# A decoder block on one core: first token tiles loaded in halves and multiplied in passes, softmax blocks taken from last to first, causal mask in the decay row

## What is computed

```
h = layer_norm(x)
hg_q, hg_f, hg_i, hg_g, fx_q, fx_k, fx_v, fx_f, gate_a, gate_b = split(h @ w_in)
y_a = hgrn2(...)            # 4 heads, a gated linear recurrence
y_b = fox(fx_q, fx_k, fx_v, fx_f)
      # 8 heads of 64: logits = q k / 8 + c[t] - c[s], c = cumsum(log sigmoid(fx_f + bias)),
      # s <= t only, softmax, times v
merged = sigmoid(gate_a) * (y_a @ w_a) + sigmoid(gate_b) * (y_b @ w_b)
h = layer_norm(alpha * h + merged @ w_o)
h = layer_norm(alpha * h + relu(h @ w_ff1)**2 @ w_ff2 + sigmoid(h @ w_pg) * (p @ w_p))
```

## Time and profile before

| what | value |
|---|---|
| runs | 1638.04 us median of 3 (1636.09 to 1638.63) |
| the profiled execution | 1637.65 us, its span 1635.8 us |
| PE, PEld | busy 1588.1 us (97%), 1325.1 us (81%) |
| DVE, ACT, POOL | busy 1150.4 us (70%), 744.0 us (45%), 694.2 us (42%) |
| DMA | 208.51 MB, mean 127 GB/s |
| chain of waits | PE 83%, DVE 5%, ACT 4%, DMA 2%, POOL 2%, issue 2% |

### The profile page before, as it was taken

How to read it: one execution, slowest core, us unless ns; L and a number is a source line. 1 busy time by engine, 2 the same in 40 slices (tenths; PEclk the granted TensorE clock), 3 DMA queues, 4 the chain that set the end, 5 groups by cost and what they waited for, 6 DMA issues and landing times.

```text
span 1635.8 us, 21111 instructions
## 1 busy us (share of the span) xinstructions
PE 1588.1 (97%) x7800; PEld 1325.1 (81%) x7800; DVE 1150.4 (70%) x1724; ACT 744.0 (45%) x1162; POOL 694.2 (42%) x487
## 2 busy tenths in 40 slices
PE   6999999999999999999999989999999999999996
PEld 4888888888888887888887868888888888888886
DVE  8558878437767668656336879986666579857977
ACT  3245454327888774511233644445444553433342
POOL 5222221522333145564443597765566323223334
PEclk9999999999999999999999999999999999999999
DMA  8211110101010143521333435554444598867672
GB/s 295 77 42 38 27 39 27 39 29 38 27 53 27 39 117 97 147 78 52 122 120 118 164 126 183 182 195 143 159 168 152 185 330 254 272 199 238 194 204 104
DMA packets 220693, 208.51 MB, mean 127 GB/s; under 512 B 9000, under 2 KB 190504, under 8 KB 218544
## 3 DMA queue, kind: packets, MB, share of 16 engines
q1 hardware_dynamic: 217424, 196.09, 38.7%
q10 hardware_dynamic: 3168, 11.08, 1.7%
HBM read 160.96 MB, written 46.17 MB: 127 GB/s over the span
## 4 chain that ended last, share of the span: by engine, by line
PE 83%; DVE 5%; ACT 4%; DMA 2%; POOL 2%; issue 2%; SPq 0%; DVEq 0%; ACTq 0%; POOLq 0%
PE dense L969 7%; PE dense L971 7%; PE dense L973 7%; PE dense L979 4%; PE dense L1315 3%; PE dense L1317 3%; PE dense L1316 3%; PE dense L1395 3%; PE dense L1396 3%; PE dense L1397 3%; PE mixA L1106 2%; PE dense L1047 2%; PE dense L1049 2%; PE dense L1048 2%; PE mixA L1315 2%
## 5 line engine op out<-in xcount | busy, mean ns | idle before, releaser
L969 PE MATMUL dense<-parts 128*128 128x512 f32 x528 | 183.3, 409 | 1.6 <-DVE page L2090 0.9
L943 POOL TENSOR_TENSOR parts<-page,parts 128x512 fp32r<-128x512 f32 x52 | 88.9, 1733 | 208.1 <-ACT parts L1909 208.1
L862 POOL TENSOR_TENSOR parts<-page,parts 128x512 fp32r<-128x512 f32 x108 | 156.3, 1469 | 44.9 <-ACT parts L1788 41.6
L971 PE MATMUL dense<-parts 128*128 128x512 f32 x528 | 174.0, 391 | 0.0
L973 PE MATMUL dense<-parts 128*128 128x512 f32 x528 | 173.3, 390 | 0.0
L854 POOL CAST parts<-page 128x1024 fp32r<-128x1024 f32 x43 | 49.3, 1145 | 287.4 <-PE dense L973 192.4
L905 POOL TENSOR_TENSOR page<-page 128x512 f32<-128x512 f32 x80 | 122.6, 1532 | 59.8 <-PE dense L1317 25.2
L913 POOL TENSOR_TENSOR parts<-page,parts 128x512 fp32r<-128x512 f32 x80 | 114.8, 1437 | 55.4 <-ACT parts L1835 50.6
L1919 ACT CAST parts<-page 128x1024 fp32r<-128x1024 f32 x56 | 58.8, 1055 | 142.8 <-DVE page L2614 123.2
L973 PEld LDWEIGHTS dense<-parts 128*128 128x128 f32 x528 | 99.1, 188 | 21.8
L971 PEld LDWEIGHTS dense<-parts 128*128 128x128 f32 x528 | 99.1, 188 | 21.0
(11 more groups left out here) (298 smaller groups left out, 4315.8 us busy)
## 6 DMA issues: line engine op xcount, KB each, us to landing
page<-in_w_ff SPq DMA_DIRECT2D x104, 512.0 KB, 6.0
page<-in_w_in SPq DMA_DIRECT2D x120, 256.0 KB, 3.2
page<-act_scratch SPq DMA_DIRECT2D x56, 512.0 KB, 5.7
act_scratch<-page SPq DMA_DIRECT2D x16, 1024.0 KB, 3.9
act_scratch<-page SPq DMA_DIRECT2D x16, 768.0 KB, 7.0
page<-in_w_o SPq DMA_DIRECT2D x32, 256.0 KB, 3.1
h_scratch<-page ACTq DMA_DIRECT2D x8, 512.0 KB, 3.5
page<-c_scratch SPq DMA_DIRECT2D x8, 512.0 KB, 5.0
```

The costliest lines, as they stand in the source:

```text
L862: ins = nc.gpsimd.tensor_tensor(R(lo, at, HALF), F(raw_page(c), at, HALF), R(hi, at, HALF).bitcast(F32), ALU.subtract)
L969: mm(o, whi, x_, start=first, stop=False)
L971: mm(o, whi, x_, start=False, stop=False)
```

## The change

It has two parts.

The start. Token tiles 0 and 1, ln0_g and ln0_b are loaded in column halves, the first half from SyncE's queue, the second from ScalarE's, ahead of all weights; weight chunks 0 and 2 then follow on SyncE's queue, 1 and 3 on ScalarE's. The first value tiles are multiplied in passes (`first_values(t, n, ks)`): n = 0 is high by high, 1 low tokens by high weights, 2 high tokens by low weights. ScalarE's order becomes: chunk 0, tile 0's high part, chunks 1 to 3, tile 1's high part, tile 2's. VectorE's low part of tile 1 moves between the two passes of tile 2's norm. The semaphores x0_in, g0_in and b0_in are others' that are used again with shifted counts.

The softmax stage. The blocks of a head go from 7 down to 0 (`block_of(G) = 7 - G % 8`), the pairs from (7, 6) down to (1, 0). The 64 mask matmuls are gone; VectorE adds the mask to the diagonal square of the decay row itself, in place, one block ahead (`mask_diagonal(G + 1)`), which fits since the blocks that follow end below that square. The exception for G % 8 == 7 on ScalarE is gone.

```diff
+def block_of(G):
+    return 7 - G % 8
 def turn_pieces(G):
-    return [(0, 4), (4, G % 8 + 1)] if G % 8 >= 5 else [(0, G % 8 + 1)]
+    i = block_of(G)
+    return [(0, 4), (4, i + 1)] if i >= 5 else [(0, i + 1)]
...
@@ SyncE
-            sp.dma_start(F(PG_X), x_t[0]).then_inc(x_in[0], 16)
+            sp.dma_start(F(PG_X, 0, HALF), x_t[0][:, 0:HALF]).then_inc(x_in[0], 16)
+            sp.dma_start(F(PG_G0, 0, HALF), row(ln0_g)[:, 0:HALF]).then_inc(g0_in, 16)
+            sp.dma_start(F(PG_B0, 0, HALF), row(ln0_b)[:, 0:HALF]).then_inc(b0_in, 16)
+            sp.dma_start(F(PG_X + 1, 0, HALF), x_t[1][:, 0:HALF]).then_inc(x_in[1], 16)
             for c in range(C_END):
+                if c in (1, 3):
+                    continue
...
-                if c == 3:
-                    for t in range(4, TT):
+                if c == 2:
+                    for t in range(2, TT):
@@ TensorE, start
+            def first_values(t, n, ks):
+                j = JOB["vhg", t]
+                out1 = dense[SET[j]][:, 0:HALF]
+                x_, base = (XHI, XLO, XHI)[n], (WHI, WHI, WLO)[n]
+                for k in ks:
+                    if t == 0 and n != 1 and k % 2 == 0:
+                        pe.wait_ge((w0_hi, None, w0_split)[n], k // 2 + 1)
+                    ins = mm(out1, R(x_ + k, t * P, P), R(base + k // 2, (k % 2) * HALF, HALF),
+                             start=n == 0 and k == 0, stop=n == 2 and k == KD - 1)
+                if n == 2 and ks[-1] == KD - 1:
+                    end(ins, j)
             turn_tokens(0)
-            for t in range(TT):
+            begin(JOB["vhg", 0])
+            pe.wait_ge(h_hi, 1)
+            first_values(0, 0, every)
+            pe.wait_ge(h_split, 1)
+            first_values(0, 1, every)
+            first_values(0, 2, range(0, 2))
+            turn_tokens(1)
+            first_values(0, 2, range(2, 4))
+            begin(JOB["vhg", 1])
+            pe.wait_ge(h_hi, 2)
+            first_values(1, 0, every)
+            pe.wait_ge(h_split, 2)
+            first_values(1, 1, every)
+            first_values(0, 2, range(4, 6))
+            turn_tokens(2)
+            first_values(1, 2, early)
+            first_values(0, 2, late)
+            first_values(1, 2, late)
+            for t in range(2, TT):
@@ TensorE, scores
-                mm(mixA[:, L - P:L], identb[:, :], causal[:, :], start=False, stop=True,
-                   ).then_inc(qk_done, 1)
@@ ScalarE, start
+            act.dma_start(F(PG_X, HALF, HALF), x_t[0][:, HALF:]).then_inc(x0_in, 16)
+            act.dma_start(F(PG_G0, HALF, HALF), row(ln0_g)[:, HALF:]).then_inc(g0_in, 16)
             act.dma_start(ident[:, :], c_ident).then_inc(ident_in, 16)
+            act.dma_start(F(PG_B0, HALF, HALF), row(ln0_b)[:, HALF:]).then_inc(b0_in, 16)
+            act.dma_start(F(PG_X + 1, HALF, HALF), x_t[1][:, HALF:]).then_inc(x1_in, 16)
+            for c in (1, 3):
+                for i in range(2):
+                    act.dma_start(F(PG_W0 + c, i * HALF, HALF), w_views["in"][:, 2 * c + i, C_HI:C_HI + HALF],
+                                  ).then_inc(w0_landed[c], 16)
@@ ScalarE, softmax
-                if 2 <= G < 66 and G % 8 == 7:
-                    high_parts(G)
                 if 1 <= G < 65:
                     divide(G)
-                if 2 <= G < 66 and G % 8 != 7:
+                if 2 <= G < 66:
                     high_parts(G)
@@ VectorE, start
-            tokens_norm(0)
-            tokens_stats(1)
-            norm_begin(F(PG_X + 1), F(PG_X + 1), 1, F(PG_G0), 1)
-            tokens_low(0)
-            norm_end(F(PG_X + 1), 1, F(PG_B0), 1).then_inc(h_ready, 1)
-            for t in range(1, TT):
+            norm_begin(F(PG_X), F(PG_X), 0, F(PG_G0), 0)
+            dve.wait_ge(b0_in, 32)
+            norm_end(F(PG_X), 0, F(PG_B0), 0).then_inc(h_ready, 1)
+            for t in range(1, 3):
+                tokens_stats(t)
+                norm_begin(F(PG_X + t), F(PG_X + t), t % 2, F(PG_G0), t)
+                tokens_low(t - 1)
+                norm_end(F(PG_X + t), t % 2, F(PG_B0), t).then_inc(h_ready, 1)
+            for t in range(2, TT):
                 if t + 1 < TT:
                     tokens_stats(t + 1)
                     tokens_norm(t + 1)
@@ VectorE, softmax
+            def mask_diagonal(G):
+                hh = G // 8
+                if G % 8 == 0:
+                    dve.wait_ge(negc_in[hh % 2], 16 * (hh // 2 + 1))
+                if G == 0:
+                    dve.wait_ge(c_ready, 1)
+                square = F(PG_NEGC[hh % 2], block_of(G) * P, P)
+                then(V.tensor_tensor(square, square, causal[:, :], ALU.add))
...
+                if G < 63:
+                    mask_diagonal(G + 1)
                 if G >= 8 and G % 8 in (1, 2) and G // 8 + 1 < NFX:
```

More of the change, by code:

```diff
@@ L1464, in _ @@
                 nc.scalar.copy(R(WHI + j), F(PG_W0 + j)).then_inc(w0_hi, 1)
-                if j == 1:
+                if j == 0:
                     tokens_high(0)
                     rstd_estimate(1)
-            for t in range(1, TT + 1):
+            rstd_estimate(2)
+            tokens_high(1)
+            rstd_estimate(3)
+            tokens_high(2)
+            store_values(PG_VHG, "vhg", 0, 0)
+            store_values(PG_VHG, "vhg", 1, 0)
+            for t in range(3, TT + 1):
                 if t + 1 < TT:
@@ L1673, in _ @@
                     act.wait_ge(pv_done, m + 1)
[L1674 removed]
+                    nc.scalar.copy(F(PG_YB[m // 8], (3 - m % 4) * 2 * P, 2 * P)[own, :], o_bank(m)[other, :]).then_inc(o_moved, 1)
                 if G >= 8 and G % 8 == 1 and G // 8 + 1 < NFX:
```

66 lines of the change are left out of this document (28 added, 38 removed).

## The result

The change makes the kernel slower: 1656.96 us in the median of 5 runs (1653.16 to 1658.42) against 1636.67 for the kernel before on the same chip, ratio 1.0119, 95% interval 1.0108 to 1.013. The direction was forecast, the size was not: +20.3 us where +4.6 was forecast, above the range of 1633 to 1648. The profiled execution took 1657.6 us (span 1655.7), 19.95 more than the one before.

What follows compares the result with a forecast made beforehand. TensorE's waits were taken as the bound: at the start, in the gate stage and in softmax operand gaps. Masks -3.5, order +6.8 and start +1.3 made +4.6 on 1637.65: 1642.2, say 1642.0 us, range 1633 to 1648.

Steps and rivals of the forecast that it cites:

- hidden by sum: Softmax stage: VectorE's mask additions, 8 x 0.3 us a head, fit its spare time, counting only where its queue is awaited.
- Masks, -3.5: Softmax stage: dropping 64 mask matmuls at 0.055 us each saves TensorE 3.5 us on the path.
- VectorE has 7 us of room in 26: One softmax head: VectorE is busy 18.6 of 26.0 us, leaving 7 us for the mask additions.
- Order of the blocks, +6.8: Softmax stage: reversed blocks meet the next head's casts, 2.0 us of stalls in six heads; 14.8 against 8.0 in all.
- each lag carried into the next step: Softmax stage, upper bound of the order term: 3.0 us of stalls a head, sum 20.8, +12.8 us.
- The exception: ScalarE's high part ahead of the division at G % 8 == 7; its removal was counted within the order term.
- The start, +1.3: Start: x lands sooner but weight casts delay the passes; value tile 2 at 35.4, taken as +1.3, bounds -0.3 to +3.
- The 3.6 us to be won at the first transposes: Start: tile 0's norm ends at 9.6 us where it ended at 13.2, 3.6 us won.
- TensorE has done its own share by 31 and waits: Start: TensorE finishes its work by 31 us, then waits for VectorE until value tile 2 starts at 35.4.
- clock rival: Start: holes between casts keep TensorE at its slow clock through both passes, tile 2 at 37, 1643.7 us; chance 0.14.
- Behind the softmax stage, 0: Stages behind softmax: the gate stage's chain shifts as a whole, no gain or loss there.

Runs made afterwards that it cites:

- hf_table_b_mask_pe: hf_table_b with the mask added by TensorE as in the kernel before; 1638.93 us, ratio 1.0011.
- hf_table_b: soft_high_first with the dense stream's passes per step (3,2,3,4,3,4,3,2) instead of three in each; 1640.79 us, ratio 1.0023.
- soft_mask_pe: soft_only with the mask added by TensorE as before, so reversed block order alone against the kernel before; 1647.61 us, ratio 1.0061.
- soft_only: The change's softmax stage with the start of the kernel before; 1651.13 us, ratio 1.0082 to the kernel before.
- fwd_add: Kernel before plus 63 additional two-input 128 x 128 VectorE operations, results unused, where the change puts its additions; 1638.45 us, ratio 1.0009.
- fwd_no_exception: Kernel before with ScalarE's division ahead of the high part in every step, also at G % 8 == 7; 1635.77 us, ratio 0.9989.
- soft_high_first: soft_only with ScalarE's high part ahead of the division at G % 8 of 3 and 5; 1644.69 us, ratio 1.0046.
- start_only: The change's start with the softmax stage of the kernel before; 1640.96 us, ratio 1.0023 to the kernel before.
- start_stats_early: start_only with tile 2's low part between the halves of tile 3's norm and tile 3's statistics ahead of tile 1's low part; 1638.71 us, ratio 1.0012.
- rev_high_first: soft_mask_pe with ScalarE's high part ahead of the division at G % 8 of 3 and 5; 1640.51 us, ratio 1.0018.

## Why the prediction was wrong
The terms of the sum, forecast and measured: order +6.8 and +10.6, additions on VectorE 0 and +5.9, masks off TensorE -3.5 and -2.4, start +1.3 and +3.9. The step that failed worst is "hidden by sum"; the others were mis-sized.

**Masks, -3.5.** Too much. Where nothing is waited for, hf_table_b_mask_pe and hf_table_b differ between the first score matmul and what follows the scores by 38, 71, 31, 40, 43 ns and twice by 0, by step: with some 80 in step 3, an estimate of 0.30 us in a head, 2.4 in all. I had taken 55 ns from a few places for all 64.

**Additions, hidden by sum.** This step failed. One alone takes 0.28 us, as taken. But they are not hidden: from soft_mask_pe to soft_only the time rises by 3.5 though TensorE is rid of an estimated 2.4, so they cost some 5.9; fwd_add shows that the same work in the old order costs 1.5. "VectorE has 7 us of room in 26" was true and beside the point. The count let an addition delay ScalarE once a head, at block 5, where the divisions of the change wait for VectorE 57 times; and in the new order TensorE soon needs what stands behind them (14.4 us of waits for the low part, against 4.9 in fwd_add).

**Order of the blocks, +6.8.** The mechanism was right, the term mis-sized: the order alone (soft_mask_pe, with TensorE's masks kept) costs 10.6. The first half of the head was right almost to the tenth: the low part ahead of the weighing of (7, 6) was forecast to follow 14.9 us behind the head's start, and in head 1, which starts at 391.86, the weighing stands at 406.91, 15.05 behind it. (TensorE waits 1.32 us there and not 2.2, since it has lost 0.41 at the turning of step 3 and comes later.) What failed is what I let follow. The count had 0.23 for the reciprocals of blocks 7 and 6 and 0.6 for block 5, where the trace has waits of 0.29, 0.23 and 0.66, and it stopped at that weighing. Block 4's division, the next one, waits 1.42 (the row at 408.21; 0.6 of it is the slowed addition), so the lag isn't given back: the weighing of (5, 4) waits too, for which I had nothing. TensorE's starts show 10.6 us ahead of the first weighing of a head, 5.6 ahead of the second, 3.0 ahead of the turnings, in eight heads. My upper bound, "each lag carried into the next step", stood for this case, and even it was passed: the 8.0 us of stalls before, the stage's +14.4 and the 2.4 of the masks make 24.8, the additions' share among them, and the bound was 20.8. I gave it the range's end and no chance.

**The exception.** I named its removal as harmful. In the old order it was worth less than nothing (fwd_no_exception, -1.2); in the new one such an exception at the right steps is worth 7.1 (6.4 with the additions).

**The start, +1.3.** Measured alone +3.9. ln0_b was taken at 9.95, forecast 7.6, so the transposes came at 11.94, not 9.6; w 0 at 12.42 (11.8), first matmul 14.98 (14.0). The 3.6 us to be won at the first transposes were 1.4 in the profiled executions. Tile 2 came at 34.26, better than the 35.4 forecast, from VectorE's idle time and tile 3's norm, as told. The step that failed is the price of waiting: "TensorE has done its own share by 31 and waits", which I wrote and costed at nothing beyond its length. The clock fell to 0.50 behind the wait, and by the end of the values the loss was 3.4 us. My clock rival had a slow stretch in the passes, not behind them. How much of the median's 3.9 is the clock is not shown: only one execution of each kernel was traced.

**Behind the softmax stage, 0.** The gate stage, as told. In the last stage the profiled execution lost 2.1 us, with one more stretch at the slow clock at 1375 us behind waits of up to 1.9 (L1434 above). soft_only and soft_high_first had one there too, the other kernels none; why it comes with these is open.

**What remains open.** The additions' slowing beside GpSimd was not taken away in any run, so how much of their 5.9 us it makes in the new order is not known; in the old order 11.2 us of it fitted into 1.5. With the high part ahead of the division the order still costs 3.5 us, and what makes them is argued, not shown. The parts sum to 18.0 and the whole to 20.3; the clock may be the rest, or the spread of the executions.

## What to carry to other kernels
Where two engines with queues in order serve each other within each step, the room that busy time leaves says little (the same work cost 1.5 us in one order and 5.9 in the other): follow every answer through both queues until the lag is gone, and if it isn't gone by the next head, the bound "carried on" is the forecast. A division that waits for another engine must not stand ahead of a copy whose input is ready and whose output the busiest engine needs; exchanging the two was worth 6 to 7 us, three tables that shuffled the busiest engine's own work no more than 4. A new idle time of TensorE of some 2 us may bring a stretch at the slow clock behind it, in some executions and not in others, and belongs in the range with its price.

## What the runs showed of the hardware
A small addition on VectorE with both inputs in SBUF took 271 to 1160 ns:

```profile
L2316 DVE TENSOR_TENSOR page<-page,causal x64: 271/284/1160, 367.1 to 584.9; 128x128 f32<-128x128 f32 x64
```

(minimum, median, maximum, and the first and last start.) 15 of the 64 took over 0.35 us, and each of them had started while a GpSimd subtraction or cast was running and ended 0.15 us behind that instruction's end. The addition at 407.10 above started in the third of GpSimd's four subtractions, which had 0.72 us left, and took 0.88. They lost 7.4 us by it in sum. The Trainium skill (SBUF — State Buffer, Who interferes with whom) states that a VectorE instruction with two SBUF inputs contends with a GpSimd instruction that reads SBUF, that the lock is exclusive, and that the order of issue decides who blocks. This trace agrees: the 15 ended 0.15 us behind the GpSimd instruction that had started first. The trace of the kernel before had no such operation in the stage, and I had looked for its price among operations with one input in PSUM.

TensorE's granted clock fell to the slow level behind an idle time of 2.57 us in the profiled execution of the change, behind 2.32 us in that of soft_only, and in the last stage of the same two behind 1.91 and 1.99 us (matmuls at 1374.24 and 1369.89). It held at the fast level through 2.29 us in that of start_only. In the gate stage nearly the same wait of 3.2 to 3.3 us stands in every kernel, and the clock fell behind it in the kernel before (at 641.8 us) and in the change, and held in fwd_no_exception and start_stats_early. So the length of the idle time alone did not decide it here. The spread of the executions doesn't tell the kernels that lose the clock from the others either: with the new start it is 4.0 to 8.0 us, and with the old one 2.3 in rev_high_first, 2.5 in fwd_no_exception, 5.6 in fwd_add and 6.7 in hf_table_b.
